# A hybrid conv/S5 mixer and a 32-expert MoE on one core: state rotations finished on GpSimd, convolution norm sums added outside TensorE, last input projection moved

## The reference

```
h = rms_norm(x) * g_mix
a_val, a_gate, u, g_conv, g_ssm = split(h @ w_in)     # 768, 768, 256, 1024, 1024 columns
v = a_val * sigmoid(a_gate)
v = causal depthwise convolution of width 31 over the rows (768 channels) + conv_b
v = silu(layer_norm(v));  y_conv = v @ w_conv_out
s_t = A * s_{t-1} + B u_t      # complex diagonal recurrence, 16 groups of 64 states
y = C s + d*u;  y = gelu(y);  y = y * sigmoid(y @ w_glu + b_glu);  y_ssm = y @ w_ssm_out
x = x + (sigmoid(g_conv)*y_conv + sigmoid(g_ssm)*y_ssm) @ w_out
h = rms_norm(x) * g_ffn
logits = h @ w_router + b_router;  top 4 of 32 experts, softmax over the four
x = x + sum over the chosen experts of gate * swiglu_expert(h)
out = rms_norm(x) * g_final
```

## Time and profile before

| what | value |
|---|---|
| median of 3 executions | 1112.43 us (1111.92 to 1113.12) |
| the profiled execution | 1112.21 us, of which the span is 1110.5 us |
| TensorE busy | 1060.8 us, 96% of the span |
| VectorE busy | 284.6 us, 26% |
| ScalarE busy | 165.6 us, 15% |
| GpSimd busy | 75.3 us, 7% |
| read from HBM | 430.58 MB, 389 GB/s over the span |

### The profile page before, as it was taken

One profiled execution on the slowest core, in us unless ns is written; L12 is line 12 of the kernel. 1 busy time (PEld: TensorE's weight loads), 2 busy tenths in 40 slices (PEclk: granted clock), 3 DMA queues, 4 the chain that ended last, 5 costly groups with the idle time before them and its releaser, 6 DMA issues.

```text
span 1110.5 us, 12064 instructions
## 1 busy us (share of the span) xinstructions
PE 1060.8 (96%) x4951; PEld 457.2 (41%) x4952; DVE 284.6 (26%) x661; ACT 165.6 (15%) x296; POOL 75.3 (7%) x153
## 2 busy tenths in 40 slices
PE   7999999999999999999999999999999999999996
PEld 6888784533333333333333333333333333333332
DVE  6999751311111111111111111111101111111112
ACT  3011301211111111111111111101001111111103
POOL 3975000000000000000000000000000000000000
PEclk9999999999999999999999999999999999999999
DMA  7853488799999999999999999999999999999995
GB/s 226 281 158 146 185 347 358 285 427 426 431 436 427 432 431 431 434 433 433 428 432 432 429 432 431 432 432 430 433 432 431 433 431 431 429 431 428 422 423 235
DMA packets 43035, 432.07 MB, mean 389 GB/s; under 512 B 5647, under 2 KB 21437, under 8 KB 24604
## 3 DMA queue, kind: packets, MB, share of 16 engines
q1 hardware_dynamic: 43004, 431.64, 92.9%
HBM read 430.58 MB, written 1.05 MB: 389 GB/s over the span
## 4 chain that ended last, share of the span: by engine, by line
PE 60%; DMA 26%; DVE 10%; ACT 1%; issue 1%; another core or an unknown queue 1%; SPq 1%; DVEq 0%
PE bank L1483 30%; DMA ring<-w_gate_up 22%; PE bank L1495 13%; DVE bank L936 6%; PE bank L1504 4%; PE bank L1445 4%; DMA ring<-w_down 3%; PE bank L1410 2%; PE bank L1375 2%; ACT area L722 1%; PE bank L1451 1%; PE bank L1476 1%; DVE bank L971 1%; DMA ring<-ssm_b_im 1%
## 5 line engine op out<-in xcount | busy, mean ns | idle before, releaser
L1483 PE MATMUL bank<-ring,area 128*64 128x512 f32 x2048 | 455.9, 602 | 22.3 <-DMA ring<-w_gate_up 22.3
L1483 PEld LDWEIGHTS bank<-ring,area 128*64 128x64 f32 x2048 | 149.4, 139 | 311.8 <-issue 272.5
L1495 PE MATMUL bank<-ring,area 128*64 128x512 f32 x1024 | 227.4, 595 | 6.1 <-ACT area L722 2.6
L1102 DVE TENSOR_SCALAR area<-bank 128x512 f32<-128x512 f32 x32 | 22.1, 692 | 732.6 <-PE bank L1483 732.6
L1495 PEld LDWEIGHTS bank<-ring,area 128*64 128x64 f32 x1024 | 72.0, 137 | 141.2 <-issue 131.7
L1264 PE MATMUL bank<-area,ring 128*128 128x256 f32 x480 | 106.6, 381 | 2.2 <-DMA ring<-w_in 2.2
L1264 PEld LDWEIGHTS bank<-area,ring 128*128 128x128 f32 x480 | 90.3, 190 | 17.1 <-DMA ring<-w_in 2.7
L728 ACT ACTIVATE area<-area 128x512 f32<-128x512 f32 x32 | 20.2, 632 | 486.9 <-DVE area L1102 486.9
L936 DVE SCALAR_TENSOR_TENSOR bank<-ring,spread,bank 128x256 f32<-128x256 f32 x174 | 71.5, 483 | 0.6
L1445 PE MATMUL bank<-rows,pick 128*64 128x512 f32 x256 | 63.6, 618 | 0.4 <-DVE onehot L1091 0.4
L1504 PE MATMUL bank<-area,spT 64*128 64x512 f32 x248 | 61.6, 615 | 0.7 <-ACT area L725 0.7
(11 more groups left out here) (243 smaller groups left out, 492.3 us busy)
## 6 DMA issues: line engine op xcount, KB each, us to landing
ring<-w_gate_up SPq DMA_DIRECT2D x47, 4096.0 KB, 48.9
ring<-w_down SPq DMA_DIRECT2D x26, 4096.0 KB, 46.6
ring<-w_gate_up SPq DMA_DIRECT2D x19, 2048.0 KB, 18.3
ring<-w_gate_up SPq DMA_DIRECT2D x30, 1024.0 KB, 12.0
ring<-w_down SPq DMA_DIRECT2D x18, 1024.0 KB, 21.2
ring<-w_in SPq DMA_DIRECT2D x15, 1024.0 KB, 8.0
ring<-w_down SPq DMA_DIRECT2D x3, 2048.0 KB, 10.8
ring<-w_out SPq DMA_DIRECT2D x1, 4096.0 KB, 14.2
```

The source lines that it names most:

```text
L1102: return v.tensor_scalar(gc, bank[4][:, :], 7.0, None, ALU.min)
L1483: last = mm(bank[4 + b][64 * h:64 * h + 64, :], heT[:, k % 4, k // 4 * 64:k // 4 * 64 + 64], fours(w, b, h), start=False, stop=(k == KD - 1))
L1495: last = mm(bank[b][64 * h:64 * h + 64, :], src[:, k % 4, k // 4 * 64:k // 4 * 64 + 64], w[:, k % 2, h * 512:h * 512 + 512], start=(k == 0 ...
```

## The change

- The scaled x itself is transposed (`x_rows`), and hT is made half by ScalarE, half by VectorE; the diagonal product is gone.
- The subtraction and the addition that end a rotation move from VectorE to GpSimd for tiles 0 to 6, with a new buffer `rot`; tile 7 stays on VectorE. GpSimd does them for tile t-1 behind its rotation of inputs for tile t.
- The states' outputs are formed in two groups of four tiles (`y_quad`), the second one before the first half of project 14.
- GpSimd adds five of the six convolution chunks; the mean takes two products. VectorE adds the squares; the variance takes one product. The second half of project 14 stands between the GLU product and the variance.
- g_ffn is multiplied into w_router by VectorE, which waits for that load before it multiplies the gates; into the gathered rows it goes at the copy of their transpose, which VectorE does in place of ScalarE. The router's small tensors lie in other memory, so that three slots of expert 1 are loaded earlier.
- x is added by VectorE in place of identity products. In the router the second row block is taken in halves, and its transposes begin inside the w_out product.
- `END` has larger pieces for experts 27 and 28.

```diff
-END = {E - 5: (4, 2, 2, 4), E - 4: (4, 2, 2, 4), E - 3: (4, 2, 1, 1, 4),
+END = {E - 4: (4, 4, 4), E - 3: (4, 2, 1, 1, 4),
-WARM = 8, 2, 6, 3
+WARM = 1, 4, 6, 3
 ...
 # SP
             sp.wait_ge(y_pe, ST)
-            (loads of gffn, wrt, brow)
+            load(1, 7, 1)
+            load(1, 8, 1)
 ...
             sp.wait_ge(biasb_ready, 1)
             sp.dma_start(wout, w_out[0].rearrange("(k p) n -> p k n", p=128)).then_inc(wout_in, 16)
+            sp.dma_start(wrt, w_router[0].rearrange("(k p) n -> p k n", p=128)).then_inc(ffn_in, 16)
+            sp.dma_start(brow, b_router.to_broadcast([128, E])).then_inc(ffn_in, 16)
+            sp.dma_start(gain[:, :], norm_ffn_g[0].rearrange("(p k) -> p k", p=128)).then_inc(ffn_in, 16)
 ...
 # GpSimd, in the loop over t, behind the rotation of the inputs
+                if t >= 1:
+                    pool.wait_ge(rot_ready, t)
+                    x_, r_ = xs[(t - 1) % NX], rot[(t - 1) % 2]
+                    g.tensor_tensor(x_[:, 0, :], x_[:, 0, :], r_[:, 1, :], ALU.subtract)
+                    g.tensor_tensor(x_[:, 1, :], x_[:, 1, :], r_[:, 0, :], ALU.add).then_inc(states, 1)
+            pool.wait_ge(conv_done, 2)
+            link(g.tensor_tensor(conv_sum, conv[:, 0, :], conv[:, 1, :], ALU.add))
+            for k in range(2, KC - 1):
+                pool.wait_ge(conv_done, k + 1)
+                last = g.tensor_tensor(conv_sum, conv_sum, conv[:, k, :], ALU.add)
 ...
 # VectorE, in the loop over t, behind the scans
+                if t >= 2:
+                    dve.wait_ge(states, t - 1)
                 v.tensor_tensor(xs[t % NX], zz, cb, ALU.mult)
-                link(v.tensor_tensor(zz, zz, sb_, ALU.mult))
-                v.tensor_tensor(xs[t % NX][:, 0, :], xs[t % NX][:, 0, :], zz[:, 1, :], ALU.subtract)
-                v.tensor_tensor(xs[t % NX][:, 1, :], xs[t % NX][:, 1, :], zz[:, 0, :], ALU.add).then_inc(states, 1)
+                v.tensor_tensor(rot[t % 2], zz, sb_, ALU.mult).then_inc(rot_ready, 1)
 ...
+            for k in range(1, KC):
+                dve.wait_ge(conv_sq, k + 1)
+                if k > 1:
+                    dve.wait_ge(sq_added, k - 1)
+                v.tensor_tensor(silu[:, 0, :], silu[:, 0, :], silu[:, k, :], ALU.add).then_inc(sq_added, 1)
 ...
             v.tensor_copy(biasb[0:32, :], bias32[0:32, :]).then_inc(biasb_ready, 1)
+            dve.wait_ge(ffn_in, 48)
+            v.tensor_tensor(wrt, wrt, gain_k.unsqueeze(2).to_broadcast([128, KD, E]), ALU.mult).then_inc(wrt_ready, 1)
 ...
+            def by_gain_T():
+                both = gain[:, :].rearrange("p (h m) -> p m h", h=2).unsqueeze(3).to_broadcast([128, 4, 2, CAP])
+                return v.tensor_tensor(heT.rearrange("p m (h c) -> p m h c", h=2),
+                                       bank[7][:, :].rearrange("p (m h c) -> p m h c", m=4, h=2), both, ALU.mult)
 ...
 # TensorE
             project(11)
-            y_pair(0)
+            y_quad(0)
             project(12)
-            y_pair(2)
             project(13)
-            y_pair(4)
+            y_quad(4)
             project(14, (0,))
-            y_pair(6)
-            pe.wait_ge(conv_done, KC)
+            pe.wait_ge(conv_done, KC + 1)
             pe.wait_ge(bu_sb, ST)
-            for k in range(KC):
-                last = mm(bank[0][:, 0:T], ones, conv[:, k, :], start=(k == 0), stop=(k == KC - 1))
-            last.then_inc(mean_pe, 1)
-            project(14, (1,))
+            mm(bank[0][:, 0:T], ones, conv[:, KC - 1, :], start=True, stop=False)
+            mm(bank[0][:, 0:T], ones, conv_sum, start=False, stop=True).then_inc(mean_pe, 1)
 ...         (GLU product)
+            project(14, (1,))
+            pe.wait_ge(sq_added, KC - 1)
+            mm(bank[1][:, 0:T], ones, silu[:, 0, :], start=True, stop=True).then_inc(var_pe, 1)
 ...
             pe.wait_ge(wout_in, 16)
-            pe.wait_ge(ffn_in, 48)
+            pe.wait_ge(wrt_ready, 1)
+            pe.wait_ge(ssm_gated, 4)
 ...
-                if j == 1:
-                    pe.wait_ge(ssm_gated, 4)
-                    for n in range(4):
-                        mm(bank[n][:, :], ident[:, :], x_sb[:, n // 2, n % 2 * 512:n % 2 * 512 + 512], start=True, stop=False)
```

More of the change, by code:

```diff
@@ L102, in build @@
         wz = [grid(at(11, 512, 1024 + 512 * i), 2, T) for i in range(2)]
+        rot = [grid(at(23, 512, 512 * i), 2, T) for i in range(2)]
         ygelu, yglu = grid(at(11, 512), 2, T), grid(at(11, 512, 512), 2, T)
         squares = grid(at(17, CH), TT, D)
+        x_rows = squares
         gateC = grid(at(17, CH), KD, T)
@@ L695, in _, with square, root_and_exp @@
                     .then_inc(silu_ready, 1)
[L697 to L708, removed]
+            def square(t, h):
+                act.wait_ge(h_ready, 2 * t + h + 1)
+                s.activation(squares_1[h], rows[:, t, 512 * h:512 * h + 512], ACT.Square,
+                             accum_out=ss4[:, 2 * t + h:2 * t + h + 1]).then_inc(x1_sq, 1)
+            def root_and_exp(t):
                 act.wait_ge(var_h, t + 1)
@@ L1286, in bu_pair, with y_quad @@
                             last.then_inc(bu_pe, 1)
-            def y_pair(t0):
-                pe.wait_ge(states, t0 + 2)
+            def y_quad(t0):
+                pe.wait_ge(states, t0 + 4)
                 for ri in range(2):
-                    for t in (t0, t0 + 1):
+                    for t in range(t0, t0 + 4):
                         r = slice(t % 4 * 32, t % 4 * 32 + 32)
@@ L1349, in _ @@
             last.then_inc(glu_pe, 1)
-            for k in range(KC):
-                pe.wait_ge(conv_sq, k + 1)
-                last = mm(bank[1][:, 0:T], ones, silu[:, k, :], start=(k == 0), stop=(k == KC - 1))
-            last.then_inc(var_pe, 1)
+            project(14, (1,))
+            pe.wait_ge(sq_added, KC - 1)
+            mm(bank[1][:, 0:T], ones, silu[:, 0, :], start=True, stop=True).then_inc(var_pe, 1)
             pe.wait_ge(y_glu, 1)
@@ new lines, in _, with out_product @@
+            pe.wait_ge(ssm_gated, 4)
+            def out_product(t, k, h):
+                pe.wait_ge(mixed, k // 2 + 1)
+                return mm(bank[2 * t + h][:, :], gateC[:, k, t * 128:t * 128 + 128], wout[:, k, h * 512:h * 512 + 512],
+                          start=(k == 0), stop=(k == KD - 1))
+            for k in range(KD):
+                for h in range(2):
+                    last = out_product(0, k, h)
+            last.then_inc(x1_pe, 1)
+            for h in range(2):
+                for k in range(KD):
+                    last = out_product(1, k, h)
+                    if h == 1 and k % 2:
+                        last.then_inc(wout_used, 1)
+                    if (h, k) == (0, 3):
+                        h2_transposes(0, 0, [(4, 0), (4, 1), (4, 2), (4, 3)])
+                        h2_transposes(0, 1, [(5, 0), (5, 1), (5, 2), (5, 3)])
+                    if (h, k) == (0, 6):
+                        pe.wait_ge(h2T_act, 1)
+                        pe.wait_ge(h2T_dve, 1)
+                        logits(0, range(KD))
+                    if (h, k) == (0, 7):
+                        last.then_inc(x1_pe, 1)
+                    if (h, k) == (1, 5):
+                        h2_transposes(1, 0, [(6, 0), (6, 1), (6, 2), (6, 3)])
@@ L1610, in _ @@
             for n in range(4):
+                residual(n)
                 down_bias(n)
             more_blocks()
-            with pe.Fori(MID // 2, E // 2 - 3) as i:
+            with pe.Fori(MID // 2, E // 2 - 2) as i:
                 for half in range(2):
                     expert(i * 2 + half, half, [i * 16 + n for n in later(half)])
-            expert(E - 6, 0, [(E // 2 - 3) * 16 + n for n in later(0)])
-            for e in range(E - 5, E - 2):
+            for e in range(E - 4, E - 2):
                 expert(e, e % 2, e)
```

295 lines of the change are left out of this document (161 added, 134 removed).

## The result

The changed kernel takes 1116.68 us (median of 6 executions, 1115.71 to 1117.34) where the kernel before takes 1112.52 (6 executions): a ratio of 1.0038, with an interval of 1.0028 to 1.0048. That is 4.2 us slower, at a forecast of 1116.0. The profiled execution took 1115.71 us, the lowest of the six and 1.0 us under their median; its span is 1114.0, so 3.5 us over the span of before.

The account below looks back on a forecast made before the run. Bound: the experts' weight stream, which starts with the first gate and up product. Mean +4.0, w_out +0.5, clock +1.7, router -2.1, copy +0.15 = +4.2 on 1112.21, 1116.4; taken 1116.0, range 1109 to 1119.

Parts of the forecast that it names:

- The end follows the first product, one to one: Experts: one microsecond at the first gate and up product is one at the end, if the 24 slots are full.
- Turn-taking at the scans: Recurrence: VectorE's scans and GpSimd's operations alternate, 1.1 us lost a tile, tile 6.84 us; chance 0.52.
- (a): Rival at the scans: no contention, a scan into PSUM shares; mean 2.8 us earlier, 1109.8 us; chance 0.22.
- (b): Rival at the scans: VectorE keeps the port for both, 0.6 lost a tile, 1112.4 us; chance 0.18.
- The mean: TensorE's mean after the second group of outputs and half project: starts at 128.5, 4.0 us later than 124.44.
- the clock term: TensorE before the mean: idling lowers the clock, bounds 0 and 1.7 us, half taken.
- From the mean to w_out: w_out starts 42.0 us after the mean, held by its load, small router loads (2.5) and VectorE's gates and mix.
- 0.5 later: Start of w_out relative to the mean: 0.5 us later than in the kernel before, though TensorE idles 7.5 us.
- Clock at w_out: TensorE's idle stretch before w_out costs clock: 1.7 us taken, bounds 0 and 3.4.
- rival (c): (a) with small loads landing with w_out (-2.5) and gather at full clock (-1.7): 1105 us; chance 0.05.
- Router and copy: Behind w_out: router 2.1 us less, 3.4 us to the logits' bias; gain at the transpose's copy costs 0.15.
- The start: Kernel's start: hT half a microsecond later and each load issued 0.3 us later, 0.3 us, counted in the mean's.

Follow-up runs that it names:

- E12: E10 with w_out loaded in one piece, late behind the bias casts: 1106.14 us, 0.9945 of the kernel before.
- E5: Changed kernel with GpSimd leaving out three of the four operations that rotate a tile's inputs (states not the reference's): 1106.38 us, 0.9949.
- E3: Changed kernel with all rotation subtractions and additions back on VectorE, the sine product kept in SBUF (rot): 1119.96 us, 1.0068.
- E9: Changed kernel with rotations wholly on VectorE as before, the sine product in PSUM (zz): 1113.86 us, 1.0017.
- E6: Changed kernel with 25 products that nobody reads put in TensorE's wait for the eighth state: 1113.06 us, 1.0011.
- E2: Changed kernel with the three small router loads issued ahead of w_out's load: 1107.34 us, 0.9954.
- E11: E10 with the rotations finished on GpSimd: 1106.58 us, 0.9949.
- E10: Changed kernel with E9's rotations, four pairs of outputs as before, small router loads and six of w_out's eight pieces early: 1103.74 us, 0.9924.
- E7: E2 with six of w_out's eight pieces also loaded far earlier: 1108.12 us, 0.9965.
- E1: Changed kernel with the second group of states' outputs behind the first half of project 14: 1115.87 us, 1.0036.
- E4: Kernel before with only the rotations of tiles 0 to 6 finished on GpSimd through rot: 1116.65 us, 1.0037.

## Why the prediction held, step by step

**The end follows the first product, one to one: right.** From it to the end of the span it is 896.7 to 898.3 us in thirteen of the fourteen kernels, over starts from 203.55 to 220.46; E12 has 899.4.

**Turn-taking at the scans: right, with its size.** A tile of 6.95 us against the 6.84 predicted and 5.64 without a meeting (E5): 1.3 us a tile instead of the 1.1 taken. The terms differ a little: the rest of L598 at the first scan is 0.96 us (92.32 - 91.36), predicted 0.7, and the second scan takes 0.5 us more than alone, as predicted. Tile 7's scans take 2.15, so 0.9 is lost there, as predicted. E3 and E9 show for the addition that it is a conflict over SBUF operands; that the scans stretch for the same reason follows from E5 and E9, where they are back at 1.27 once no GpSimd operation runs beside them, but no run gave a scan other operands. Rivals (a) and (b) are gone: a scan into PSUM does not share, and VectorE does not keep its turn for both scans, since L599 runs before the second has ended (92.40 to 93.39, scans to 93.94). The rule of the Trainium skill that the prediction cited ("SBUF — State Buffer", section "SBUF: two separate sides": an exclusive lock for a whole instruction, against a VectorE operation with two SBUF inputs) is borne out by E3's 1.49 against E9's 0.41 us.

**The mean: 5.6 us later, predicted 4.0.** The eighth state came at 123.72 (predicted 123.2), as the tile was a tenth of a microsecond longer than thought. The rest of the miss is the clock term: half of 1.7 us was taken, but the group and the half project both ran at 1.2 GHz, 0.87 and 0.8 us, which is the whole 1.7. E6 gives the same price from the other side (1.8).

**From the mean to w_out: 40.6 us, predicted 42.0.** `biasb_ready` 20.8 us after the mean (predicted 21.0), w_out landed at 35.1 (35.2), the small loads at 36.2 (37.7), VectorE's part 4.4 (4.3). So the step was right in kind, and the 2.5 us for the small loads were too many; 1.1 are measured. Its mechanism was not quite the one argued: the prediction had three loads waiting behind w_out in the queue, and the last one was not in the queue at all, because SP stood 8.68 us at the one before it. A row of the kernel before could have said so: of the 9.1 us of ssm_b_im, the prediction's upper bound for w_router, 4.25 are SP's issue. TensorE idled 5.93 us before w_out, predicted 7.5. E2 shows what stands behind the sum's "0.5 later": the wait eats 8.0 us that the change had earned elsewhere.

**Clock at w_out: 2.2 us, predicted 1.7** (E2's 43.07 against 45.30).

**The gather: not in the sum.** It ran at full clock, 1.94 for 3.58 us, which gave back 1.6. The prediction had this only inside rival (c). It nearly cancels the two clock terms that were too small (0.8 and 0.5), and that is luck. For those two terms the forecast was even set 0.6 us below its sum, "as the two clock terms are near their upper bounds together"; each was half of its bound, and both came out above what was taken.

**Router and copy: right.** From w_out's last result to the logits' bias it is 207.00 - 203.68 = 3.3 us (3.4). From w_out to the first product the kernel needs 45.30 us, and needed 46.76: -1.46 = +2.2 (clock) - 1.6 (gather) - 2.0. The -2.0 is what is left over, and stands against a predicted -2.1 + 0.15.

**The start: 0.3 at the recurrence,** whose first scan is at 71.81, as predicted.

In all: +5.57 - 0.95 - 1.46 = +3.16 us at the first product (the second is 40.57 less the 41.52 of before), +3.5 on the span, +4.2 between the medians; predicted +4.2. The sum was nearer than its terms: a trace that shows +3.2 does not confirm 4.2, and the profiled execution was the fastest of six. What the runs do confirm is the mechanism. The worth of the parts against the changed kernel, each by its ratio: rotations 2.3 us (E9) or 2.8 (E11 less E10), small loads 9.3 (E2), w_out early 2.4 (E12 less E10). They don't add, because each wait that goes uncovers the next: E7 gained nothing over E2 by the same early load.

## What to carry to other kernels

Before an operation is handed from VectorE to GpSimd, look at where its neighbours' operands lie: two operands in SBUF against a GpSimd operation means one after the other, and with one operand in PSUM the addition was free of it (0.41 against 1.49 us). A wait on small loads behind a large one has to be costed with the issuing queue, not with the sizes: put a load in many short pieces where its engine has time, with nothing urgent behind it. When TensorE is made to wait, add the clock for the work behind the wait (0.8 to 2.6 us a time here, behind waits of 2.3 us and more), and count on the next wait appearing where one is removed.

## What was not expected of the hardware

- SP stood 8.68 us in the issue of a 16 KB load in the changed kernel, 10.97 in E2 and 12.31 in E10, behind w_router's 1024 pieces of 128 bytes on queues with megabytes of large loads before them (DMA share 1.00 to 1.03 in E2 from 135 to 147; in the changed kernel 0.40 in 150 to 153, then 0.99 to 1.03). With 1 KB pieces on empty queues the same issue took 0.43. Large loads alone do not do it: the kernel before issues loads of 1 MB right behind w_out's 4 MB in at most 1.29 us each (DMA share 0.99 in 150 to 153). The same kernel does stand once the pieces are short: 4.25 and 3.77 us at its start, behind loads of 1024 pieces (ssm_b). So the short pieces are needed, as far as these runs show; whether they would be enough on empty queues was not tried. The Trainium skill ("DMA: Bandwidth & Descriptors", section "Issuing engines are not separate DMA queues") calls the sequencer's time to initiate a DMA usually small against the DMA itself; here it was not, as the 8.68 us are two thirds of the 12.8 from b_router's issue to its landing. SP's timeline in the kernel before, for the two comparisons:

```profile
8.61 4.25 SPq L364 DMA_DIRECT2D ring<-ssm_b_im  x1
152.22 1.29 SPq L388 DMA_DIRECT2D ring<-w_gate_up  x1
```

- An addition of 256 columns takes 0.41 us or 1.49, by one operand's place alone, while GpSimd works (E9, E3).
- The clock falls at shorter waits than the prediction had in mind: around 3.04 us in E1 (the GLU product 3.05 for 1.89 us; behind the 3.21 just before it not yet) and 3.01 in E4 (5.49 for 2.86), and behind 2.30 in E12 (1.19 for 0.59); behind the 2.00 of E10 it did not (granted clock 1.00 in 123 to 129).
